# The order of silu, product and weight splits in the expert steps of a decoder kernel

## The chip, the cores and the metric

The kernel runs on one core of a Trainium2 chip. The metric is the device time of one execution in microseconds (us); less is better. Its engines are TensorE (PE, matmul), VectorE (DVE), ScalarE (ACT), GpSimd (POOL) and SyncE (SP), each with a queue of instructions of its own that it works off in order. Semaphores join them.

## The reference

The model is a decoder trunk of two layers for 256 tokens of width 1024, in fp32. Each layer has a mixer, a cross attention and a feed-forward part. The feed-forward part of the second layer is a mixture of 8 experts, of which each token uses two. The change touches only that part:

```python
def swiglu(x, w1, w2):
    gate, up = jnp.split(x @ w1, 2, axis=-1)
    return (jax.nn.silu(gate) * up) @ w2

def moe_ffn(x, router_w, w1, w2):
    ...
    logits = (xt @ router_w).astype(jnp.float32)
    top_logit, top_idx = lax.top_k(logits, TOP_K)
    gates = jax.nn.softmax(top_logit, axis=-1)
    ...
    yb = lax.map(expert_group, (xb, blk_expert)).reshape(cap, d)
    yb = yb * slot_gate[:, None].astype(yb.dtype)
```

An expert's hidden width is 2816, so its weights are 22 chunks of the first product (w1) and 11 of the second (w2), each 128 x 2048 fp32, 1 MB. All 8 experts are 264 chunks.

## The kernel before

**Split weights.** TensorE multiplies fp32 numbers as a sum of products of a high and a low part. ScalarE copies a chunk (`raw`, `kvX`, `arena`) to its high part in one of four homes, three buffers `whi` and one `whi_fourth` (L820, `split_high`). VectorE subtracts this from the chunk and writes the low part over the chunk (L1949, `split_low`). SP's queue loads the chunks into 9 slots. A slot, and a home, come free when TensorE has used the chunk (`w_used`). Some chunks are taken whole, in unsplit fp32 matmuls, and need neither engine.

**Pairs, units and steps.** The experts go in 4 pairs of one full expert (up to 128 tokens, H) and one light expert (up to 64 tokens, L). Each expert is a row of 22 units: units 0 to 10 take two chunks of w1 each and produce gate and up for 256 hidden columns, units 11 to 21 take one chunk of w2. `turns()` gives the steps: in a step comes a unit of the full expert and then the unit of the light expert that stands three behind (LAG), so steps 0 to 2 of a later pair still hold units 19 to 21 of the light expert of the pair before, and the first pair has none there. Chunks are taken whole in the full expert only: the second chunk of units 4, 5, 6, 8 and 9, and the chunks of units 11 to 13. Where this text speaks of step 7, the full expert's unit is 7.

**Splits run four ahead.** The split of a chunk can begin when TensorE is done with the split chunk four places before it in the stream, whose home it takes. `splits_through(n)` issues the splits that follow on the chunks up to n:

```python
while done[0] < NSPLIT and (done[0] < HOMES or SPLIT[done[0] - HOMES] <= n):
    split_high(p, done[0])
    done[0] += 1
```

So in a step ScalarE and VectorE have up to two splits that follow on the full unit's chunks, and up to two that follow on the light unit's.

**What else is in a step.** For the full unit ScalarE makes the silu of the gate half (L1159, `xsilu`), which waits until TensorE has done both chunks of the unit, and VectorE multiplies it by the up half (L2535, `xgated`). TensorE transposes the product behind the next unit (L1762), ScalarE and VectorE copy and split the result (L1131 and L1134, `hidden_hi`; L2505, `hidden_lo`). For the light unit the high and low rows of the 128 come out of the array apart: ScalarE copies the low rows (L1172), VectorE adds them to the high ones (L2552, `lsum`), ScalarE makes the silu of the sum (L1125, `light_silu`) and VectorE the product (L2497, `light_gated`). The two last belong to the step after (`behind`). The transposes of the light product are L1775. At step 1 of the first pair the light expert's tokens are gathered by TensorE (L1619) and copied out (L1100, `first_hi_of("L")`). At steps 5 and 7 of the later pairs TensorE spreads the outputs of the pair before (L1673, L1674) and VectorE adds them to h (L2519). At the end of a light expert ScalarE and VectorE write the high and low part of its output (L1178, L2559).

**TensorE's lines.** The split product of the full expert is L1249 to L1251, 12 matmuls of 512 columns for a chunk of w1; a whole chunk is L1714, 8 matmuls; the light expert's chunk is L1711 and L1712, 8 matmuls, and L1748 and L1749 in its second product. `ready(n)` waits for the low part of a chunk (`lo_ready`).

Of the kernel before, what the change touches and what calls it, by code (L numbers as in the profile page):

```python
# [69 lines left out]
def unit_chunks(u):  # L70
    return (2 * u, 2 * u + 1) if u < NF // 2 else (W1_CHUNKS + u - NF // 2,)
# [87 lines left out]
def build(nc, x, mem, par, con, lvl, lin_w, ffn_w, out):  # L159
# [31 lines left out]
    with ExitStack() as ctx:  # L191
# [546 lines left out]
        def _(act):  # L738
# [340 lines left out]
            def experts(p):  # L1079
# [3 lines left out]
                def splits_through(n):  # L1083
# [4 lines that stand above are left out]
# [57 lines left out]
                    act.wait_ge(routed_ok, 1)  # L1145
                behind = None
                for a, (full, light) in enumerate(turns()):
                    if full:
                        i, u = full
                        splits_through(SIDX["H", i, unit_chunks(u)[-1]])  # L1150
                    if a == 1:
                        first_hi_of("L")
                    if behind:
                        light_silu(*behind)
                        behind = None
                    if full:
                        if u < NF // 2:
                            act.wait_ge(w_used, unit_end(p, "H", i, u))
                            nc.scalar.activation(xsilu[:, u % 2, :], pb[:, u % 2, 0:S], ACT.Silu).then_inc(silu_ready, 1)  # L1159
                        if 1 <= u <= NF // 2:  # L1160
                            hidden_hi(i, u - 1)
                        if u == UNITS - 1:
                            act.wait_ge(selT_ready, nth(p, i))
                            act.wait_ge(w_used, unit_end(p, "H", i, u))
                            nc.scalar.activation(yHh.rearrange("p (a c) -> p a c", a=2), pb[:, 1:3, :], ACT.Copy,
                                                 scale=gs[:, 0:1]).then_inc(yH_hi, 1)
                    if light:
                        i, u = light
                        splits_through(SIDX["L", i, unit_chunks(u)[-1]])
                        if u < NF // 2:  # L1170
                            act.wait_ge(w_used, unit_end(p, "L", i, u))
                            nc.scalar.activation(low_rows[0:LIGHT, :], pb[LIGHT:P, 3 + u % 2, :], ACT.Copy).then_inc(low_ready, 1)  # L1172
                            behind = light
                        if 2 <= u <= NF // 2 + 1:
                            light_hidden_hi(i, u - 2)
                        if u == UNITS - 1 and i < PAIRS_E - 1:
                            act.wait_ge(w_used, unit_end(p, "L", i, u))
                            nc.scalar.activation(yLh.rearrange("p (a c) -> p a c", a=2), pb[:, 4:6, :], ACT.Copy,  # L1178
                                                 scale=gs[:, 1:2]).then_inc(yL_hi, 1)
                    if full:  # L1180
                        i, u = full
                        if u == 9:
                            selections_turned(i)
                        if u in (15, 18) and i < PAIRS_E - 1:
                            gathered_hi(i + 1, (u - 15) // 3)
# [667 lines left out]
        def _(dve):  # L1853
# [616 lines left out]
            def experts(p):  # L2470
# [3 lines left out]
                def splits_through(n):  # L2474

                    while done[0] < NSPLIT and (done[0] < HOMES or SPLIT[done[0] - HOMES] <= n):
                        split_low(p, done[0])
                        done[0] += 1
# [42 lines left out]

                behind = None
                for a, (full, light) in enumerate(turns()):
                    if full:
                        i, u = full
                        splits_through(SIDX["H", i, unit_chunks(u)[-1]])
                    if a == 1:
                        first_lo_of(p, "L")
                    if behind:
                        light_gated(*behind)  # L2530
                        behind = None
                    if full:
                        if u < NF // 2:
                            dve.wait_ge(silu_ready, full_no(p, i, u))
                            V.tensor_tensor(xgated[:, u % 2, :], xsilu[:, u % 2, :], pb[:, u % 2, S:2 * S],  # L2535
                                            ALU.mult).then_inc(g_ready, 1)
                        if 1 <= u <= NF // 2:
                            hidden_lo(i, u - 1)
                        if u == UNITS - 1:
                            dve.wait_ge(yH_hi, nth(p, i))  # L2540
                            V.scalar_tensor_tensor(out=yHl.rearrange("p (a c) -> p a c", a=2), in0=pb[:, 1:3, :],
                                                   scalar=gs[:, 0:1],
                                                   in1=yHh.rearrange("p (a c) -> p a c", a=2).bitcast(F32),
                                                   op0=ALU.mult, op1=ALU.subtract).then_inc(yH_lo, 1)
# [140 lines left out]
```

## Time and profile before

| | |
|---|---|
| time, median of 3 runs | 1419.19 us (1417.68 to 1422.4) |
| the profiled execution | 1417.29 us, span 1415.1 us |
| PE busy | 1384.8 us (98%), 7443 matmuls |
| VectorE busy | 1107.9 us (78%) |
| ScalarE busy | 909.9 us (64%) |
| splits of VectorE in the experts (L1949 wlo<-raw,whi alone) | 73, 2282 ns each |
| loads in the experts | 1024 KB each, 7.5 to 8.0 us from issue to landing |
| granted clock of TensorE over the span | 0.996 |

The span runs from the first to the last instruction; the profiled execution's time is 2.2 us longer. The experts take the second half, from about 709 us to 1407 us. Times of a single instruction are those from its start to its end; instructions of one engine overlap by some 0.1 us, so the distance from one start to the next is shorter than what an instruction takes. A matmul of 512 columns is written as taking 0.39 us and more, while the next starts 0.23 us later.

### The profile page before, as it was taken

To read this page: it belongs to the slowest core of one execution; us is meant where nothing else is said; L and a number is where in the kernel's file an instruction comes from. 1 tells how busy PE (TensorE), PEld (TensorE's weight loads), DVE (VectorE), ACT (ScalarE), POOL (GpSimd) and SP (SyncE) were. 2 spreads that over 40 slices of the span, in tenths; PEclk is the share of its full clock that TensorE was granted. 3 is DMA by queue.
4 is the path that set the end of the run, shared out by engine and by line. 5 is a ranking of instruction groups with operands and counts; after the bars stand their busy time and mean duration, and the time that the engine had idled before them with its cause. 6 is when DMAs were issued, how large, how long until landed. Compare 5 with 4: busy or idle time off the path is not lost.

```text
span 1415.1 us, 18950 instructions
## 1 busy us (share of the span) xinstructions
PE 1384.8 (98%) x7443; PEld 1139.5 (81%) x7443; DVE 1107.9 (78%) x1187; ACT 909.9 (64%) x1008; POOL 52.3 (4%) x58
## 2 busy tenths in 40 slices
PE   7999999999999999999999999999999999999997
PEld 7999898888888998989776768777687767877775
DVE  7868665666645787865588889988899888998897
ACT  6746444555534756344467778877788777877775
POOL 0031000000000022000000000000000000000000
PEclk9999999999999999999999999999999999999998
DMA  8433453455555443353569999999999999999993
GB/s 312 160 127 118 151 177 113 156 179 188 198 181 188 172 146 104 135 178 126 231 240 401 400 400 405 423 402 380 405 404 423 399 376 411 403 423 399 378 414 150
DMA packets 54480, 388.36 MB, mean 274 GB/s; under 512 B 6000, under 2 KB 6256, under 8 KB 8176
## 3 DMA queue, kind: packets, MB, share of 16 engines
q1 hardware_dynamic: 53840, 384.98, 70.3%
q10 hardware_dynamic: 544, 2.10, 0.4%
q8 instruction: 61, 1.00, 0.3%
q14 instruction: 35, 0.29, 0.1%
HBM read 386.00 MB, written 1.05 MB: 274 GB/s over the span
## 4 chain that ended last, share of the span: by engine, by line
issue 51%; PE 47%; DVE 2%; DMA 0%; ACT 0%; POOL 0%; POOLq 0%; DVEq 0%
PE pb L1249 10%; PE pb L1250 10%; PE pb L1251 10%; PE pb L1545 5%; PE pb L1546 3%; PE pb L1397 1%; PE pb L1479 1%; PE pb L1499 1%; PE pb L1230 1%; PE pb L1548 1%; DVE xTb L1919 1%; DMA h<-in_x 0%; PE pb L1489 0%; PE pb L1455 0%; PE pb L1456 0%
## 5 line engine op out<-in xcount | busy, mean ns | idle before, releaser
L1870 DVE TENSOR_TENSOR wlo<-raw,whi 128x2048 fp32r<-128x2048 f32 (+1 forms) x101 | 225.9, 2246 | 107.6 <-ACT whi L750 107.3
L750 ACT ACTIVATE whi<-raw 128x2048 fp32r<-128x2048 f32 (+1 forms) x101 | 189.9, 1882 | 148.9 <-PE pb L1251 116.0
L820 ACT ACTIVATE whi<-raw 128x2048 fp32r<-128x2048 f32 x91 | 172.7, 1913 | 42.3 <-PE pb L1251 29.7
L1949 DVE TENSOR_TENSOR wlo<-raw,whi 128x2048 fp32r<-128x2048 f32 x73 | 165.3, 2282 | 16.8 <-ACT whi L820 16.6
L1249 PE MATMUL pb<-xTb,whi 128*128 128x256 f32 x384 | 110.0, 287 | 1.8 <-DVE xTb L1907 1.2
L1545 PE MATMUL pb<-xTb,whi 128*128 128x512 f32 x308 | 111.0, 399 | 0.2
L1250 PE MATMUL pb<-xTb,whi 128*128 128x256 f32 x384 | 108.6, 283 | 0.0
L1251 PE MATMUL pb<-xTb,wlo 128*128 128x256 f32 x384 | 108.6, 283 | 0.0
L1711 PE MATMUL pb<-whi,xg 128*128 128x512 f32 x264 | 107.1, 406 | 0.0
L1949 DVE TENSOR_TENSOR kvXr<-kvX,whi 128x2048 fp32r<-128x2048 f32 x42 | 95.4, 2282 | 12.1 <-ACT whi L820 12.1
L1546 PE MATMUL pb<-xTb,wlo 128*128 128x256 f32 x352 | 91.6, 281 | 0.0
L820 ACT ACTIVATE whi<-kvX 128x2048 fp32r<-128x2048 f32 x42 | 79.9, 1914 | 16.6 <-PE pb L1251 11.6
L1249 PE MATMUL pb<-whi,xTb 128*128 128x512 f32 (+1 forms) x224 | 86.0, 384 | 0.7 <-DVE xTb L1919 0.6
L820 ACT ACTIVATE whi<-arena 128x2048 fp32r<-128x2048 f32 x41 | 78.0, 1914 | 12.0 <-PE pb L1712 5.3
L1251 PE MATMUL pb<-whi,xTb 128*128 128x512 f32 (+1 forms) x224 | 84.2, 376 | 0.0
L1250 PE MATMUL pb<-wlo,xTb 128*128 128x512 f32 (+1 forms) x224 | 84.1, 376 | 0.0
L1249 PE MATMUL pb<-whi,xg 128*128 128x512 f32 x208 | 82.2, 395 | 0.0
L1251 PE MATMUL pb<-whi,xg 128*128 128x512 f32 x208 | 81.2, 390 | 0.0
L820 ACT ACTIVATE whi_fourth<-raw 128x2048 fp32r<-128x2048 f32 x34 | 65.1, 1914 | 20.2 <-PE pb L1251 10.4
L1249 PEld LDWEIGHTS pb<-xTb,whi 128*128 128x128 f32 x384 | 73.6, 192 | 2.5 <-issue 1.7
L1250 PEld LDWEIGHTS pb<-xTb,whi 128*128 128x128 f32 x384 | 73.6, 192 | 0.1
L1251 PEld LDWEIGHTS pb<-xTb,wlo 128*128 128x128 f32 x384 | 73.6, 192 | 0.0
(459 smaller groups left out, 3488.0 us busy)
## 6 DMA issues: line engine op xcount, KB each, us to landing
raw<-in_ffn_w SPq DMA_DIRECT2D x179, 1024.0 KB, 7.5
raw<-in_lin_w SPq DMA_DIRECT2D x64, 1024.0 KB, 4.9
kvX<-in_ffn_w SPq DMA_DIRECT2D x60, 1024.0 KB, 8.0
arena<-in_ffn_w SPq DMA_DIRECT2D x58, 1024.0 KB, 8.0
raw<-in_lin_w SPq DMA_DIRECT2D x4, 536.0 KB, 5.5
arena<-in_mem ACTq DMA_DIRECT2D x2, 1024.0 KB, 8.1
h<-in_x SPq DMA_DIRECT2D x1, 1024.0 KB, 5.2
out<-xn SPq DMA_DIRECT2D x2, 512.0 KB, 4.0
```

The costliest lines, as they stand in the source:

```text
L750: nc.scalar.activation(whi[:, m % HRING, c], raw[:, m % RING, c], ACT.Copy).then_inc(hi_ready, 1)
L820: nc.scalar.activation(high_home(p, n), xraw_slots[slot], ACT.Copy).then_inc(hi_ready, 1)
L1230: mm = nc.tensor.transpose(pb[:, turn_bank(no, b), i * S + t * P:i * S + (t + 1) * P], xn[:, t, k * P:(k + 1) * P], ident)
L1249: nc.tensor.matmul(o, lh, rh, start=first, stop=False)
L1250: nc.tensor.matmul(o, lh, rl, start=False, stop=False)
L1251: return nc.tensor.matmul(o, ll, rh, start=False, stop=last)
L1397: mm = nc.tensor.matmul(pb[:, b + hd % 2, i * P:(i + 1) * P], K[r, o + t * P:o + (t + 1) * P], Q[r, o + t * P:o + (t + 1) * P], start=True ...
L1545: nc.tensor.matmul(o, high, xTb[:, :, k, :], start=(k == 0), stop=False)
L1546: mm = nc.tensor.matmul(o[:, 0:S], low, xTh[:, k, :], start=False, stop=False)
L1711: nc.tensor.matmul(o, both, w[0][:, kk, :], start=first, stop=False)
L1870: V.tensor_tensor(wlo[:, m % RING, c], raw[:, m % RING, c], whi[:, m % HRING, c].bitcast(F32), ALU.subtract).then_inc(lo_ready, 1)
L1949: V.tensor_tensor(xlo_slots[slot], xraw_slots[slot], high_home(p, n).bitcast(F32), ALU.subtract).then_inc(lo_ready, 1)
```

## The change

In the loop over the steps, on ScalarE and on VectorE, the splits that follow on the full unit's chunks stood first. They now stand behind the full unit's silu (on VectorE: its product). Whatever stood between comes ahead of them too: at step 1 the first gather's parts for the light expert, and in all steps with something `behind`, the light silu and the light product. The splits that follow on the light unit's chunks stay where they were. TensorE, SP and POOL have the same instructions in the same order.

```diff
@@ ScalarE @@
                 for a, (full, light) in enumerate(turns()):
-                    if full:
-                        i, u = full
-                        splits_through(SIDX["H", i, unit_chunks(u)[-1]])
                     if a == 1:
                         first_hi_of("L")
                     if behind:
                         light_silu(*behind)
                         behind = None
                     if full:
+                        i, u = full
                         if u < NF // 2:
                             act.wait_ge(w_used, unit_end(p, "H", i, u))
                             nc.scalar.activation(xsilu[:, u % 2, :], pb[:, u % 2, 0:S], ACT.Silu).then_inc(silu_ready, 1)
+                        splits_through(SIDX["H", i, unit_chunks(u)[-1]])
                         if 1 <= u <= NF // 2:
                             hidden_hi(i, u - 1)
@@ VectorE @@
                 for a, (full, light) in enumerate(turns()):
-                    if full:
-                        i, u = full
-                        splits_through(SIDX["H", i, unit_chunks(u)[-1]])
                     if a == 1:
                         first_lo_of(p, "L")
                     if behind:
                         light_gated(*behind)
                         behind = None
                     if full:
+                        i, u = full
                         if u < NF // 2:
                             dve.wait_ge(silu_ready, full_no(p, i, u))
                             V.tensor_tensor(xgated[:, u % 2, :], xsilu[:, u % 2, :], pb[:, u % 2, S:2 * S],
                                             ALU.mult).then_inc(g_ready, 1)
+                        splits_through(SIDX["H", i, unit_chunks(u)[-1]])
                         if 1 <= u <= NF // 2:
                             hidden_lo(i, u - 1)
```

ScalarE at the start of the experts, steps 0 and 1 of the first pair, before. L820 is a split, L1159 the full unit's silu, L1100 the parts of the light expert's gather, L1131 the copy of the transposed product.

```order
L820 ACTIVATE whi_fourth<-raw 128x2048
L820 ACTIVATE whi<-raw 128x2048 x2
L1159 ACT_TABLE_LOAD
L1159 ACTIVATE xsilu<-pb 128x256
L820 ACTIVATE whi<-arena 128x2048
L820 ACTIVATE whi_fourth<-arena 128x2048
L1100 ACTIVATE xg<-pb,params 128x64 x8
L1159 ACTIVATE xsilu<-pb 128x256
L1131 ACTIVATE arena<-pb 128x256
```

The same place of ScalarE after the change; the silu is now L1157, and its number in the file alone has changed.

```order
L1157 ACT_TABLE_LOAD
L1157 ACTIVATE xsilu<-pb 128x256
L820 ACTIVATE whi_fourth<-raw 128x2048
L820 ACTIVATE whi<-raw 128x2048 x2
L1100 ACTIVATE xg<-pb,params 128x64 x8
L1157 ACTIVATE xsilu<-pb 128x256
L820 ACTIVATE whi<-arena 128x2048
L820 ACTIVATE whi_fourth<-arena 128x2048
L1131 ACTIVATE arena<-pb 128x256
```

The first silu, with the table load ahead of it, has moved up past the three splits of step 0. The two splits of step 1 (`whi<-arena`, `whi_fourth<-arena`) have moved down past the gather's parts and the silu.

ScalarE at step 7 of the first pair, before. L1172 and L1140 end the step before it, L820 with `raw_77` and `kvX` are the two splits that follow on the full unit's chunks, L1125 is the light silu.

```order
L1172 ACTIVATE arena<-pb 64x512
L1140 ACTIVATE xhL<-pb 128x2x64
L820 ACTIVATE whi_fourth<-raw_77 128x2048
L820 ACTIVATE whi<-kvX 128x2048
L1125 ACTIVATE arena<-arena 64x256
L1159 ACTIVATE xsilu<-pb 128x256
L1134 ACTIVATE xhTh<-pb 128x256
L820 ACTIVATE whi<-raw 128x2048 x2
L1172 ACTIVATE arena<-pb 64x512
L1140 ACTIVATE xhL<-pb 128x2x64
```

The same place after the change, where the copy of the low rows is L1171.

```order
L1171 ACTIVATE arena<-pb 64x512
L1140 ACTIVATE xhL<-pb 128x2x64
L1125 ACTIVATE arena<-arena 64x256
L1157 ACTIVATE xsilu<-pb 128x256
L820 ACTIVATE whi_fourth<-raw_77 128x2048
L820 ACTIVATE whi<-kvX 128x2048
L1134 ACTIVATE xhTh<-pb 128x256
L820 ACTIVATE whi<-raw 128x2048 x2
L1171 ACTIVATE arena<-pb 64x512
L1140 ACTIVATE xhL<-pb 128x2x64
```

Both silus now stand ahead of the two splits, and the splits of the light unit (`raw`, x2) stand where they stood.

VectorE at step 7 of the first pair, before. L2552 is the light sum of the step before, L1949 a split, L2497 the light product, L2535 the full unit's product, L2505 the low part of the transposed product.

```order
L2552 TENSOR_TENSOR arena<-arena,pb 64x512
L2511 TENSOR_TENSOR xhL<-pb,xhL 128x2x64
L1949 TENSOR_TENSOR raw8r<-raw_77,whi_fourth 128x2048
L1949 TENSOR_TENSOR kvXr<-kvX,whi 128x2048
L2497 TENSOR_TENSOR arena<-arena 64x256
L2535 TENSOR_TENSOR xgated<-xsilu,pb 128x256
L2505 TENSOR_TENSOR xhTl<-pb,xhTh 128x256
L1949 TENSOR_TENSOR wlo<-raw,whi 128x2048 x2
L2552 TENSOR_TENSOR arena<-arena,pb 64x512
```

The same place after the change; these lines are now L2550, L1948, L2496, L2532 and L2504.

```order
L2550 TENSOR_TENSOR arena<-arena,pb 64x512
L2510 TENSOR_TENSOR xhL<-pb,xhL 128x2x64
L2496 TENSOR_TENSOR arena<-arena 64x256
L2532 TENSOR_TENSOR xgated<-xsilu,pb 128x256
L1948 TENSOR_TENSOR raw8r<-raw_77,whi_fourth 128x2048
L1948 TENSOR_TENSOR kvXr<-kvX,whi 128x2048
L2504 TENSOR_TENSOR xhTl<-pb,xhTh 128x256
L1948 TENSOR_TENSOR wlo<-raw,whi 128x2048 x2
L2550 TENSOR_TENSOR arena<-arena,pb 64x512
```

The two products have come ahead of the two splits.

## Rows read from the trace of the kernel before

In the timelines a row gives start and duration in us, and in brackets how long the engine had been idle and what ended that.

**Rows 1.** Busy time by window; then PEclk, DMA share, GB/s

```profile
721.20:724.40 3.20, 3.17 (x8) 2.50 (x9) 3.20 (x2) 3.17 (x3) 0.00 (x0) 0.50 1.02 430
726.00:1407.00 681.00, 678.51 (x2880) 507.29 (x2880) 613.35 (x528) 523.64 (x513) 0.26 (x1) 1.00 0.97 390
```

**Rows 2.** Waits, 726 to 1407 us. Who waited for whom: us, times, longest

```profile
PE pb L1762 <- DVE xgated L2535: 0.2, 1, 0.2
```

**Rows 3.** Timeline, first steps: start, us, engine, line, [idle <-releaser]

```profile
715.37 1.92 ACT L820 ACTIVATE whi_fourth<-raw 128x2048 fp32r<-128x2048 f32 x1 [4.20 <-DVE small L2440]
...
720.90 1.28 ACT L1159 ACT_TABLE_LOAD   x1
...
718.89 2.28 DVE L1949 TENSOR_TENSOR wlo<-raw,whi_fourth 128x2048 fp32r<-128x2048 f32 x1
...
715.20 0.39 PE L1249 MATMUL pb<-whi,xg 128*128 128x512 f32 x1
...
721.23 0.79 PE L1249 MATMUL pb<-whi_fourth,xg 128*128 128x512 f32 x1 [3.14 <-DVE wlo L1949]
```

**Rows 4.** Timeline, steps 1 to 4 of the first pair

```profile
729.93 1.75 ACT L1100 ACTIVATE xg<-pb,params 128x64 fp32r<-128x64 f32 x8 [2.18 <-PE pb L1619]
...
735.44 0.48 PE L1249 MATMUL pb<-whi,xg 128*128 128x512 f32 x1
...
741.07 0.38 PE L1762 MATMUL pb<-consts,xgated 128*128 128x128 f32 x2
...
744.94 0.39 PE L1249 MATMUL pb<-whi,xg 128*128 128x512 f32 x1
```

**Rows 5.** Timeline, the end of step 7 of the first pair, and step 8

```profile
781.82 1.92 ACT L820 ACTIVATE whi<-kvX 128x2048 fp32r<-128x2048 f32 x1 [0.81 <-PE pb L1251]
783.64 0.40 ACT L1125 ACTIVATE arena<-arena 64x256 f32<-64x256 f32 x1
...
784.47 3.71 ACT L820 ACTIVATE whi<-raw 128x2048 fp32r<-128x2048 f32 x2
...
792.09 0.42 ACT L1125 ACTIVATE arena<-arena 64x256 f32<-64x256 f32 x1 [1.18 <-DVE arena L2552]
...
783.77 2.29 DVE L1949 TENSOR_TENSOR kvXr<-kvX,whi 128x2048 fp32r<-128x2048 f32 x1 [0.29 <-ACT whi L820]
...
786.98 4.48 DVE L1949 TENSOR_TENSOR wlo<-raw,whi 128x2048 fp32r<-128x2048 f32 x2
791.38 0.67 DVE L2552 TENSOR_TENSOR arena<-arena,pb 64x512 f32<-64x512 f32 x1
...
781.55 0.39 PE L1762 MATMUL pb<-consts,xgated 128*128 128x128 f32 x2
...
785.84 0.50 PE L1249 MATMUL pb<-whi_fourth,xg 128*128 128x512 f32 x1
```

**Rows 6.** Timeline, steps 0 to 4 of the second pair

```profile
887.63 1.92 ACT L820 ACTIVATE whi<-raw 128x2048 fp32r<-128x2048 f32 x1 [0.72 <-PE pb L1251]
...
889.18 0.39 PE L1249 MATMUL pb<-whi,xg 128*128 128x512 f32 x1
...
902.24 0.38 PE L1762 MATMUL pb<-consts,xgated 128*128 128x128 f32 x2
...
904.30 0.39 PE L1249 MATMUL pb<-whi,xg 128*128 128x512 f32 x1
...
909.75 0.38 PE L1762 MATMUL pb<-consts,xgated 128*128 128x128 f32 x2
...
913.65 0.39 PE L1249 MATMUL pb<-whi,xg 128*128 128x512 f32 x1
...
909.19 1.28 DVE L2559 SCALAR_TENSOR_TENSOR yLl<-pb,route,yLh 128x1024 fp32r<-128x1024 f32 x1
```

**Rows 7.** Timeline, another gap of TensorE

```profile
105.81 1.17 PE L1397 MATMUL pb<-arena 64*128 64x128 f32 x17
108.10 1.16 PE L1397 MATMUL pb<-arena 64*128 64x128 f32 x15 [1.13 <-DVE arena L2143]
```

## The prediction

> **What bounds the kernel now.** I read the busy time by window first. Over 681 us of the experts, TensorE is busy for 678.5 us at the full clock, while VectorE has work for 613 us of it and ScalarE for 524 us [rows 1]. A busy share is not yet a bound, so the waits came next: from 726 us to the end of the experts TensorE waits once for another engine, 0.2 us, and that is the product that the change brings forward [rows 2]. Last came the timeline. Ahead of this stretch is the one real wait of TensorE, 3.1 us before 721.23, for the low part of a weight chunk [rows 3]. ScalarE, VectorE and the loads feed TensorE just in time, and nobody sees them. So in the experts a change can take away at most these waits, and whatever makes TensorE wait anew is paid in full.
>
> **What the change moves.** No instruction is added or removed. Three things come ahead of the splits of the full expert's chunks: the light expert's silu and product left from the step before, the full expert's own silu and product, and at step 1 the parts of the light expert's first gather. The silu waits for the last matmul of the full expert's unit. The first split of the step waited only for the unit's first chunk, one chunk (2.7 to 3.4 us) earlier. Now ScalarE holds it behind the silu. No DMA stands in the moved code: SP's queue waits for TensorE alone, and POOL has nothing here.
>
> **What the silu itself brings.** The product is wanted by the transposes that follow the next unit of the full expert, almost a step later. The bound on the gain is the 0.2 us that TensorE waits for it once [rows 2]. I take 0.2 us, and it is in the first term below.
>
> **What the late splits cost.** First the durations. A release by TensorE is seen by ScalarE 0.27 us after the next matmul's start (781.55 to 781.82). A split is handed to VectorE after 1.92 + 0.03 us (781.82 to 783.77). Small operations of ScalarE follow each other 0.28 us apart (three of them from 783.64 to 784.47). VectorE's splits follow each other 2.20 us apart (two from 786.98 to 791.38) and one lasts 2.29 us; between 783.77 and 786.98 stand one split and three small operations, so these take 0.34 us each. VectorE's sum for the light expert lasts 0.67 us, and ScalarE sees it 0.04 us later (791.38 to 792.09) [rows 5]. TensorE starts 0.06 us after VectorE's split ends (718.89 + 2.28 = 721.17 to 721.23) [rows 3].
>
> So the first split of a step is ready, at the earliest, 0.27 + 0.28 + 1.92 + 0.03 + 2.29 + 0.06 = 4.85 us after the end of the full unit. The splits run four split chunks ahead, since there are four homes for high parts. Where no chunk between is taken whole, the fourth one on comes up soon. I went through the steps and asked when each is wanted; U is the end of the full unit, and the lag is what TensorE has lost so far.
>
> First pair, steps 0 and 1. ScalarE comes at 715.37 and sees the end of unit 0 (715.20) at 715.47. Table load (1.28), silu (0.28) and the split (1.92) end at 718.95, and VectorE is busy with the routing until 718.89. Its product of 0.34 us now stands ahead of the split that TensorE waits for: some 0.3 us more at 721.23 [rows 3]. The 0.2 us wait for the product behind unit 1 goes away. Lag 0.1 us.
> First pair, step 1. The two splits now stand behind the parts of the gather, which wait for TensorE until 729.93. Eight parts (1.6 us), lag, silu (0.27) lead to 731.9; the first split is ready 1.92 + 0.04 + 2.28 + 0.06 us later, at 736.2. Unit 3 wants it at 735.44 + 0.1 [rows 4]. Stall 0.65 us, lag 0.75.
> First pair, step 3. Ready at U + 4.85, wanted by unit 4 at U + 3.87 (741.07 to 744.94) [rows 4]. Stall 1.0 us, lag 1.7.
> First pair, step 7. Here it is no longer U that decides. ScalarE's light silu waits for VectorE's sum, and that is the end of VectorE's work for the step before; the next splits stand behind it. Both engines so work in series: 0.04 + 0.28 + 0.28 + 1.92 + 0.03 = 2.55 us from the sum's end to VectorE's first split, then 3 splits (6.6), one small operation (0.34) and the sum (0.67): 10.2 us a step with three splits. In step 3 VectorE's first split starts at 741.07 + 0.75 + 2.50 = 744.3 and four splits and the sum lead to 753.8. Steps 4, 5 and 6 end with the sum at 784.3. The first split of step 7 is ready at 784.3 + 2.55 + 2.29 + 0.06 = 789.2; unit 8 wants it at 785.84 + 1.7 = 787.55 [rows 5]. Stall 1.65 us. Step 10 also has four splits, but three whole chunks follow and its first split is wanted a step later: no stall.
> First pair: 0.1 + 0.65 + 1.0 + 1.65 = 3.4 us.
>
> Each later pair, step 0. U is 887.63 - 0.27 = 887.36. The second chunk of unit 1 is wanted half a unit (5.45 / 2, 904.30 to 909.75) after 889.18, at U + 4.55; ready at U + 4.85. Stall 0.3 us.
> Each later pair, steps 2 and 3. Step 2 has three splits and the low part of the previous light expert's output. With U = 902.24 + 0.3, VectorE's first split starts at 905.04, three splits end at 911.64, the low part (1.28 - 0.08) at 912.84, the product of step 3 (0.34) at 913.18, the split at 915.46: ready 915.5. Unit 4 wants it at 913.65 + 0.3 [rows 6]. Stall 1.55 us. In steps 5 and 7 TensorE also spreads outputs, 8 matmuls ahead of the next unit, and that covers step 7's split.
> Each later pair 1.85 us, three of them: 5.5 us.
>
> Sum: 3.4 + 5.5 = 8.9 us. The profiled execution took 1417.3 us, so it would take 1426.2; the median of the three runs is 1.9 us above it, so the forecast is 1419.2 + 8.9 = **1428.1 us**. The runs shown spread over 4.7 us, and about 0.3% (4.3 us) is what a measurement can tell from no change.
>
> The bounds: if every chain is 0.3 us shorter than I think, the nine stalls (3 in the first pair, 2 in each other) lose 2.7 us: 1425.4. If each is 0.3 us longer, and step 2's first split in the later pairs stalls as well (U + 4.85 again, 907.4, and its need half a unit after 904.30 + 0.3, 907.3), it is 1432.
>
> **The rivals.**
> Series pace (15%). The chain of step 7 holds in the later pairs too, and step 10's reaches TensorE. For it speaks that VectorE has 90% of work already, so idle time is hard to make up [rows 1]; against it the 1.9 us of cover that spreading gives. Another 1.65 us at step 7 of three pairs and up to 1 us at step 10 of four: +9, 1437.
> The clock (8%). After the 3.1 us wait the granted clock was 0.50 for 3.2 us: 8 matmuls filled it, 0.40 us each, where 24 take 5.45 us (904.30 to 909.75), 0.23 each: 1.4 us lost [rows 1, 3, 6]. If the five stalls of 1 us and more cost this too, it is 5 x 1.4 = 7 more, 1435. Against it: after a gap of 1.13 us, 15 matmuls took 1.16 us, the pace of the 17 before it, 1.17 us [rows 7]. My stalls lie nearer to the 1.13 than to the 3.1. The Trainium skill (TensorE: Matmul & The Clock Gate, Part 1) has it that the clock is full or half according to how busy TensorE has just been; the trace agrees with both levels, 1.00 (2.4 GHz) and 0.50 (1.2 GHz), and that rule speaks against any change that opens gaps in a full queue.
> Absorbed, not slower (14%). The weight stream may be what really sets the pace: the loads fill 0.97 of the DMA time at 390 GB/s. Then late matmuls only use up time that loads would have cost, and it stays at 1419. It decides if the stream can go no faster; against it, TensorE waits for no load, and for 3.2 us the stream did 430 GB/s, 10% more [rows 1, 2]. Slack of 0.3 us at each hand-over and 1.7 at step 7 would do it as well.
> Faster (4%). The silu brings back more than the late splits cost. There is 0.2 us of wait to take away in the experts, and the 3.1 us wait ends with VectorE's routing; 1415 would need matmuls that run closer together.
>
> **How the numbers follow.** Forecast 59%: 1424 to 1432. Series 15%, clock 8%, absorbed 14%, faster 4%. The range goes from the top of the absorbed case up to the costly ones: 1422 to 1436. It leaves out most of "absorbed", "faster", and the upper half of "series", some 2 in 10. Slower by over 0.3% (above 1423.5): forecast, series, clock and a little less, 0.81. Within: 0.15. Faster: 0.04.
>
> **What would show it.** In the trace after, TensorE should show new waits for VectorE's low parts, behind units 2, 3 and 7 of the first pair and behind units 0 and 3 of the other three, 9 us in all, against 3.3 us now with the one at 721 us still there. ScalarE should wait longest for the unit's end ahead of the silu and for VectorE's sum ahead of the light silu, no longer ahead of the splits. The clock should stay at 1.00. I am wrong if the waits are there and the time is not, if they stand at other steps, or if they are of another size.

## The result

The changed kernel takes 1438.8 us (median of 4 runs, 1438.4 to 1442.7) against 1419.3 us before; the ratio is 1.0144, with a 95% interval of 1.0122 to 1.0165. It is slower by 19.5 us. The forecast was slower by 8.9, with a range that ended at 1436.

The page of the profile after, its span, its busy times and the group that has changed most:

```profile
span 1437.0 us, 18951 instructions
...
PE 1392.0 (97%) x7443; PEld 1140.1 (79%) x7443; DVE 1109.9 (77%) x1187; ACT 902.6 (63%) x1008; POOL 52.3 (4%) x58
...
L1125 ACT ACTIVATE arena<-arena 64x256 f32<-64x256 f32 x44 | 18.4, 417 | 126.6 <-DVE arena L2550 126.6
```

The span is 21.9 us longer (1437.0 against 1415.1), while VectorE and ScalarE do the same work. What ScalarE's light silu (L1125) waits for VectorE has become the longest wait of that engine in the experts. From 726 us to their end, before and after (engine, line, waited for: us, times, longest):

```profile
ACT arena L1125 <- DVE arena L2552: 35.9, 19, 3.0
...
ACT arena L1125 <- DVE arena L2550: 126.6, 44, 3.8
```

The splits stand behind this silu in ScalarE's queue now and are held with it. Their own waits for TensorE have fallen from 84.6 to 16.5 us. VectorE and TensorE over the stretch of [rows 1] (columns as there):

```profile
726.00:1407.00 681.00, 666.78 (x2798) 492.82 (x2797) 596.37 (x514) 504.93 (x499) 0.00 (x0) 0.99 0.98 388
```

TensorE is busy for 666.8 us of the 681 where it was for 678.5. Its waits up to 1429 us, where there was one of 0.2 us [rows 2]:

```profile
PE pb L1248 <- DVE kvXr L1948: 3.3, 3, 1.3
PE pb L1774 <- DVE xhL L2510: 3.0, 4, 0.8
PE pb L1248 <- DVE wlo L1948: 2.4, 2, 1.3
PE pb L1248 <- DVE raw7r L1948: 2.4, 2, 1.3
PE pb L1248 <- DVE raw8r L1948: 1.8, 1, 1.8
PE pb L1248 <- DVE raw6r L1948: 1.2, 1, 1.2
```

These are 13 waits, 14.1 us. L1248 is the full expert's matmul; L1774 are the light expert's transposes. Where they stand is read in the timeline, of which these are the waits of the first pair and one of the second, behind the one that was there before (start, us, engine, line, idle before and what ended it):

```profile
721.83 0.50 PE L1248 MATMUL pb<-whi_fourth,xg 128*128 128x512 f32 x1 [3.45 <-DVE wlo L1948]
...
747.79 0.47 PE L1248 MATMUL pb<-whi,xg 128*128 128x512 f32 x1 [0.82 <-DVE kvXr L1948]
...
790.63 0.47 PE L1248 MATMUL pb<-whi_fourth,xg 128*128 128x512 f32 x1 [1.77 <-DVE raw8r L1948]
...
832.72 0.30 PE L1774 MATMUL pb<-consts,arena 64*128 64x64 f32 x2 [0.76 <-DVE xhL L2510]
...
870.48 0.47 PE L1248 MATMUL pb<-whi_fourth,xhTh 128*128 128x512 f32 x1 [1.11 <-DVE kvXr L1948]
...
924.23 0.47 PE L1248 MATMUL pb<-whi,xg 128*128 128x512 f32 x1 [1.26 <-DVE wlo L1948]
```

747.79 is the start of unit 4, which began at 744.94 before [rows 4], 790.63 that of unit 8, before 785.84 [rows 5], and 924.23 that of unit 4 in the second pair, before 913.65 [rows 6]. So TensorE is 2.85, 4.8 and 10.6 us late at these three places. The starts at 832.72 (the light transposes of step 11) and 870.48 (unit 18) are waits that the prediction does not have.

I set the same matmuls of both traces side by side to see how the 21.9 us come about. Unit 4 loses 1.0 us in the first pair and 1.45 in each other, 5.4; unit 8 of the first pair 1.7; the transposes of step 11 lose 0.8 in each pair, 3.2; unit 18 loses 1.2 to 1.4 in each, 5.1; units 0 to 3 of the later pairs lose 0.6 each, 1.8; the start 0.3. Two stretches at the half clock cost 3.0 (below). That is 20.5 us; the rest is spread in small pieces, 0.3 us of it ahead of the experts. All this holds for the two profiled executions; one of the two stretches does not come in each execution (last section).

### The profile page after: what moved, and what is told of

Same layout as the page of the kernel before. It is cut to its first block, busy times and chain, and to the rows that moved or that the text cites. A ratio compares the mean times of both kernels' runs of the same rounds, so it can differ in the third digit from the quotient of the medians.

```text
span 1437.0 us, 18951 instructions
## 1 busy us (share of the span) xinstructions
PE 1392.0 (97%) x7443; PEld 1140.1 (79%) x7443; DVE 1109.9 (77%) x1187; ACT 902.6 (63%) x1008; POOL 52.3 (4%) x58
## 4 chain that ended last, share of the span: by engine, by line
issue 51%; PE 44%; DVE 2%; DMA 1%; ACT 0%; POOL 0%; POOLq 0%; DVEq 0%; ACTq 0%
PE pb L1248 10%; PE pb L1250 9%; PE pb L1249 9%; PE pb L1544 5%; PE pb L1545 3%; PE pb L1396 1%; PE pb L1478 1%; PE pb L1498 1%; PE pb L1547 1%; DMA arena<-in_mem 1%; PE pb L1229 1%; DVE xTb L1918 1%; DVE wlo L1869 0%; DMA h<-in_x 0%; PE pb L1488 0%
## 5 line engine op out<-in xcount | busy, mean ns | idle before, releaser
L1948 DVE TENSOR_TENSOR wlo<-raw,whi 128x2048 fp32r<-128x2048 f32 x73 | 164.9, 2284 | 17.1 <-ACT whi L820 17.1
L820 ACT ACTIVATE whi<-raw 128x2048 fp32r<-128x2048 f32 x91 | 171.9, 1908 | 5.9 <-PE pb L1250 5.8
L1248 PE MATMUL pb<-xTb,whi 128*128 128x256 f32 x384 | 110.2, 287 | 2.4 <-DVE xTb L1906 1.2
L1948 DVE TENSOR_TENSOR kvXr<-kvX,whi 128x2048 fp32r<-128x2048 f32 x42 | 95.4, 2285 | 11.6 <-ACT whi L820 11.6
L1125 ACT ACTIVATE arena<-arena 64x256 f32<-64x256 f32 x44 | 18.4, 417 | 126.6 <-DVE arena L2550 126.6
L1248 PE MATMUL pb<-whi,xg 128*128 128x512 f32 x208 | 83.9, 403 | 4.7 <-DVE kvXr L1948 2.1
L1248 PE MATMUL pb<-whi,xTb 128*128 128x512 f32 (+1 forms) x224 | 85.8, 383 | 0.7 <-DVE xTb L1918 0.6
L820 ACT ACTIVATE whi<-kvX 128x2048 fp32r<-128x2048 f32 x42 | 79.5, 1908 | 4.0 <-PE pb L1250 3.9
L820 ACT ACTIVATE whi<-arena 128x2048 fp32r<-128x2048 f32 x41 | 77.7, 1910 | 0.3 <-PE pb L1250 0.3
L1248 PEld LDWEIGHTS pb<-xTb,whi 128*128 128x128 f32 x384 | 73.6, 192 | 3.3 <-issue 2.5
L1948 DVE TENSOR_TENSOR wlo<-raw,whi_fourth 128x2048 fp32r<-128x2048 f32 x28 | 64.0, 2286 | 13.3 <-ACT whi_fourth L820 13.3
```

What stands on the lines that cost most here:

```text
L820: nc.scalar.activation(high_home(p, n), xraw_slots[slot], ACT.Copy).then_inc(hi_ready, 1)
L1125: nc.scalar.activation(lsilu[0:LIGHT, :], lsum[0:LIGHT, 0:S], ACT.Silu).then_inc(lsilu_ready, 1)
L1248: nc.tensor.matmul(o, lh, rh, start=first, stop=False)
L1948: V.tensor_tensor(xlo_slots[slot], xraw_slots[slot], high_home(p, n).bitcast(F32), ALU.subtract).then_inc(lo_ready, 1)
```

## The experiments

Each kernel was timed beside the kernel before on the same chip. In what follows a ratio is to that kernel, with its interval; 0.01 is 14.2 us. The changed kernel itself was not timed again beside them, so "less than the changed kernel" is the difference of two ratios, each known to some 2 to 4 us. Differences of 5 us and less are therefore not sure by the times alone; what the text says of single waits rests on the traces. U is the end of the full unit, as in the prediction.

**1. One engine at a time.** Two kernels: ScalarE has the changed order and VectorE the old one, and the other way round.

```diff
 # ScalarE alone: VectorE's loop keeps
+                    if full:
+                        i, u = full
+                        splits_through(SIDX["H", i, unit_chunks(u)[-1]])
                     if a == 1:
                         first_lo_of(p, "L")
```

> ScalarE has the changed order, VectorE the old one (its splits first, then the products). Theory A (the high parts are late: on ScalarE the first split of a step stands behind the unit's end and behind VectorE's light sum): nearly the whole loss, as the low parts cannot start before the high ones; only the 0.3 to 0.7 us of the two products ahead of VectorE's splits are saved at each stall, so 12 to 19 us over before. Theory B (VectorE, the fuller engine, stands idle for its products ahead of its splits): at most 5 us over before.

Measured: 1465.2 us, ratio 1.0324 (1.0291 to 1.0357), 46 us more than before. Neither theory had that. TensorE's waits from 709 us on, its largest:

```profile
PE pb L1761 <- DVE xhTl L2504: 6.5, 4, 2.1
PE pb L1774 <- DVE arena L2496: 6.4, 4, 1.7
...
PE pb L1761 <- DVE xgated L2534: 5.0, 2, 4.8
...
PE pb L1774 <- DVE xhL L2510: 3.3, 3, 1.1
```

With VectorE's splits in front, its products stand behind splits whose high parts are late, and then TensorE waits for the products themselves (L2496, L2534) and for the low part of the transposed product (L2504). Of the four lines shown, the changed kernel has only the wait for the copy of the light transposes (L2510).

> VectorE has the changed order, ScalarE the old one. Theory A as such, that only late high parts matter: at most 5 us over before. Theory B: most of the loss or more, since VectorE's splits now stand behind a product whose silu follows on both high splits of the step: first low part ready at U + 5.7 us instead of U + 4.85 (U is the full unit's end), 15 to 30 us over before.

Measured: 1444.0 us, ratio 1.0165 (1.0135 to 1.0196), 26 us by the medians. That is the range of theory B, and theory A's bound of 5 us falls. But B falls by the first run. ScalarE's order alone costs more than twice what the two together do; VectorE's alone costs about the same as both (its interval, 1.0135 to 1.0196, overlaps 1.0122 to 1.0165). The reading is that the products and the splits should stand in the same order on both engines, because each hands work to the other in that order; the first run shows it for the old order on VectorE alone. The loss cannot be put down to one engine.

**2. One half of the change at a time.** The full expert's silu and product ahead of the splits, everything else behind them; and the reverse.

```diff
 # the full expert's alone, ScalarE (VectorE likewise)
                     if full:
                         i, u = full
+                        if u < NF // 2:
+                            act.wait_ge(w_used, unit_end(p, "H", i, u))
+                            nc.scalar.activation(xsilu[:, u % 2, :], ...
                         splits_through(SIDX["H", i, unit_chunks(u)[-1]])
                     if a == 1:
                         first_hi_of("L")
                     if behind:
                         light_silu(*behind)
```

> Only the full expert's silu and product stand ahead of the splits, the light ones and the first gather's parts stay behind them, on both engines. If the two mechanisms are apart (the wait for the unit's end delays the first split of a step; the light silu's wait for VectorE's sum puts both engines in series): new waits of TensorE ahead of unit 4 in all pairs (1.0 to 1.5 us), unit 8 of the first pair (0.6) and in unit 1 of the later pairs (0.3), none ahead of the light expert's transposes of step 11 and none ahead of unit 18; 6 to 9 us over before. If one backlog makes all stalls, they stay where they are in the changed kernel and the loss is over 14 us.

Measured: 1430.6 us, ratio 1.0080 (1.0055 to 1.0104), 11 to 13 us more than before. TensorE's waits:

```profile
PE pb L1777 <- DVE xhL L2513: 4.3, 4, 1.1
PE pb L1251 <- DVE kvXr L1951: 2.1, 2, 1.3
PE pb L1251 <- DVE raw7r L1951: 1.3, 1, 1.3
```

The waits ahead of unit 4 are there (0.81 us in the first pair, 1.30 in the second) and ahead of unit 8 (0.51), and none ahead of unit 18. But the transposes of step 11 wait too, 1.1 us each, where the expectation had none, and the loss is above its 6 to 9 us. So the full expert's silu alone is enough for this wait.

> Only the light silu and product, and the first gather's parts at step 1, stand ahead of the splits; the full expert's silu and product stay behind. If the series of the two engines is a mechanism of its own: waits of TensorE ahead of the transposes of step 11 and ahead of unit 18 in every pair, none ahead of unit 4, and 5 to 10 us over before. If the light silu does harm only together with the full one: under 3 us.

Measured: 1428.6 us, ratio 1.0069 (1.0042 to 1.0095). TensorE's waits:

```profile
PE pb L1764 <- DVE xgated L2537: 3.0, 1, 3.0
PE pb L1777 <- DVE xhL L2513: 1.1, 1, 1.1
PE pb L1251 <- DVE kvXr L1951: 1.1, 1, 1.1
```

The waits ahead of unit 18 are there (1.10 us in the first pair, 0.58 to 0.72 in the others) and none ahead of unit 4, as expected. Unit 8 of the first pair waits 0.39. Ahead of the transposes of step 11 there is one only, in the first pair. A new one of 3.0 us stands at step 1: the gather's parts are ahead of the splits, and the product of unit 1 is behind them. The two halves are mechanisms of their own in units 4 and 18. The sum 0.0080 + 0.0069 = 0.0149 is near the 0.0144 of the whole, but not because the places add up: the wait of 3.0 us is in the light half alone, step 11 waits in both, and unit 8 waits 0.51 and 0.39 apart and 1.8 together.

**3. The places, one by one.** These kernels are the changed one with the old order put back at some steps, on both engines. The condition differs: step 14; step 10; step 2; steps 0 (of the later pairs), 3 (of all) and 7 (of the first); those with 14 and the copy of step 11 first as well; and steps 0, 2, 3, 7, 10 and 14.

```diff
                 for a, (full, light) in enumerate(turns()):
+                    if full and full[1] == 14:    # or other steps
+                        splits_through(SIDX["H", full[0], unit_chunks(full[1])[-1]])
                     if a == 1:
```

> The changed kernel, but at step 14 alone the full unit's split stands ahead of the light silu and product, as before the change. If the light silu at step 14 starts the lateness that reaches unit 18: the four waits of 1.2 to 1.4 us ahead of unit 18 go, 5 us less than the changed kernel (1.1% over before in place of 1.4%). If they come from the backlog of steps 10 to 13, they stay and so does the time.

Measured: ratio 1.0109 (1.0081 to 1.0138), 5.0 us less than the changed kernel's 1.0144. The waits ahead of unit 18 are gone in all four pairs, those of unit 4, unit 8 and step 11 stand as they were. In the changed kernel step 14 looks like this in the first pair, ScalarE first and then VectorE:

```profile
854.78 0.42 ACT L1125 ACTIVATE arena<-arena 64x256 f32<-64x256 f32 x1 [2.42 <-DVE arena L2550]
855.11 1.90 ACT L820 ACTIVATE whi_fourth<-arena 128x2048 fp32r<-128x2048 f32 x1
...
857.04 2.29 DVE L1948 TENSOR_TENSOR raw6r<-arena,whi_fourth 128x2048 fp32r<-128x2048 f32 x1 [1.32 <-ACT whi_fourth L820]
...
866.26 1.88 DVE L2486 SCALAR_TENSOR_TENSOR xg<-pb,params,xg 128x128 fp32r<-128x128 f32 x8
868.06 2.28 DVE L1948 TENSOR_TENSOR kvXr<-kvX,whi_fourth 128x2048 fp32r<-128x2048 f32 x1
```

L1125 at 854.78 is the light silu, which had waited 2.4 us for the sum, and the split of step 14 follows at 855.11. VectorE has it at 857.04, and from there on its splits and the gather's low parts (L2486) follow each other without a gap up to the split at 868.06. Its end at 870.34 is what unit 18 waits for. Four steps lie between the cause and the wait.

> The changed kernel, but with the old order at step 10 alone, the step with four splits ahead of the waits of step 11. If VectorE's backlog that shows at steps 11, 12 and at unit 18 begins here: the waits of step 11 go and the ones ahead of unit 18 shrink too, 4 to 7 us less than the changed kernel. If it has built up over steps 4 to 9: the waits stay, time within 1 us of the changed kernel.

Measured: ratio 1.0113 (1.0098 to 1.0129), 4.4 us less. The waits of step 11 are gone, and the ones ahead of unit 18 are down from 1.1 or 1.2 us to between 0.2 and 0.4. The backlog begins at step 10. It and step 14 both have to be in the new order for unit 18 to lose its full 1.3 us: step 10 put back takes away 0.8 to 0.9 of it, step 14 put back all. This is step 10 of the first pair in the changed kernel:

```profile
820.34 0.38 ACT L1157 ACTIVATE xsilu<-pb 128x256 f32<-128x256 f32 x1 [0.83 <-PE pb L1250]
...
832.41 0.42 ACT L1125 ACTIVATE arena<-arena 64x256 f32<-64x256 f32 x1 [3.30 <-DVE arena L2550]
...
822.56 4.49 DVE L1948 TENSOR_TENSOR wlo<-raw,whi 128x2048 fp32r<-128x2048 f32 x2 [1.38 <-ACT whi L820]
826.97 0.42 DVE L2504 TENSOR_TENSOR xhTl<-pb,xhTh 128x256 fp32r<-128x256 f32 x1
827.30 2.28 DVE L1948 TENSOR_TENSOR raw6r<-arena,whi_fourth 128x2048 fp32r<-128x2048 f32 x1
...
831.71 0.67 DVE L2550 TENSOR_TENSOR arena<-arena,pb 64x512 f32<-64x512 f32 x1
832.30 0.27 DVE L2510 TENSOR_TENSOR xhL<-pb,xhL 128x128 fp32r<-128x128 f32 x1
```

Unit 10's silu starts at 820.34, the first of four splits reaches VectorE at 822.56, the sum follows at 831.71 and the copy of the light transposes (L2510) ends at 832.57. TensorE's next transposes want that copy, and start at 832.72.

> The changed kernel, but at step 10 the copy of the light expert's transposes (ScalarE's high part, VectorE's low part) stands ahead of the light unit's splits and not behind them and the light sum. It takes away what TensorE waits for ahead of the light transposes of step 11. If each stall is a deadline of its own: the four waits of 0.8 us go, 3 us less than the changed kernel. If VectorE carries one backlog from step 10 to unit 18: the waits of step 11 go and those ahead of unit 18 grow by as much, no change in time against the changed kernel (within 1 us).

Measured: ratio 1.0145 (1.0125 to 1.0166), no gain. The edit makes the copy that step 11 waits for ahead of the splits of the light unit 7 (shown on ScalarE, VectorE likewise):

```diff
+                        if u == 7:    # u is the light unit
+                            light_hidden_hi(i, u - 2)
...
-                        if 2 <= u <= NF // 2 + 1:
+                        if u != 7 and 2 <= u <= NF // 2 + 1:
```

The four waits of step 11 went, but they did not show up ahead of unit 18 either. They came one step later, at the transposes of step 12, and are longer:

```profile
PE pb L1776 <- DVE xhL L2512: 4.6, 4, 1.2
```

The waits ahead of unit 18 stayed at 1.1 to 1.2 us. So neither reading came true as it stands. The deadline is no single one: VectorE is late as a whole, and here what was brought forward in its queue put off the copy of the next step.

> The changed kernel, but with the old order (the splits first) at step 3 of all pairs, step 7 of the first and step 0 of the others, the places where the prediction had its stalls. If they are what was forecast there: the waits ahead of unit 4, of unit 8 in the first pair and in unit 1 go, with the slow clock behind unit 8's: 1.0 + 1.7 + 1.5 + 3 x 1.8 = 9.6 us less than the changed kernel. The waits of step 11 and unit 18 stay.

Measured: ratio 1.0090 (1.0070 to 1.0111), 7.7 us less, where 9.6 were expected. In the first pair unit 4 and unit 8 no longer wait. In the later pairs unit 4 still waited 0.94 to 0.99 us of its 1.3 (the 1.1 in the next expectation is too high), although step 3 had the old order.

> The changed kernel, but with the old order at step 2 of the later pairs alone. The earlier run with the old order at step 3 still had TensorE wait 1.1 us ahead of unit 4 in the later pairs. If that wait is made in step 2 (VectorE starts its three splits and the low part of the light output late and hands the lateness on): the three waits ahead of unit 4 in the later pairs shrink from 1.25 us to under 0.5, 3 to 4 us less than the changed kernel. If both steps make it alone (either is enough): they stay above 1 us and the time falls by less than 1 us.

Measured: ratio 1.0138 (1.0122 to 1.0153), 0.9 us less. The waits ahead of unit 4 in the later pairs shrank to about 0.8 us. Either of steps 2 and 3 makes most of the wait alone, so the second reading is the nearer one.

> The three edits (copy first at step 10, old order at step 14, old order at steps 0, 3 and 7) together. If the places named are all: 17 to 18 us less than the changed kernel, 2 us over before, of which 1.5 are the clock at 730 us. If stalls taken away only come back at other steps, it stays at 5 us or more over before, with new waits.

Measured: ratio 1.0073 (1.0050 to 1.0096), 10 us less, not 17. The transposes of step 12 wait 1.2 us in each pair, and unit 4 in the later pairs 1.0. That is the second reading: what the copy's new place took away at step 11 came back at step 12.

> The changed kernel, but with the old order at steps 2, 3, 10 and 14 of every pair, step 7 of the first and step 0 of the others, so at every step where a wait was traced to. If these steps are the whole cause: 0 to 2 us over before, of it up to 1.5 us the half clock near 730 us, and no wait of 1 us behind step 3. If each reordered step leaves some lateness that VectorE hands on: 4 us or more over before, with waits at steps that had none.

Measured: ratio 1.0021 (1.0003 to 1.0040), 3 us over before. The shortest runs, 1421.5 against 1417.5 us, are 4.0 apart, and the profiled executions 4.4 (spans of 1419.5 and 1415.1 us). TensorE's waits, of which the first holds the one of 3.1 us that was there before (now 3.5):

```profile
PE pb L1250 <- DVE wlo L1950: 3.9, 2, 3.5
...
PE pb L1763 <- DVE xgated L2536: 0.3, 1, 0.3
```

No wait of 1 us is left behind step 3. Of the 4.4 us about 1.5 are the half clock near 730 us, 0.5 the wait for the product of step 2 at 743.29 us, and 2.0 unit 4 of the later pairs, which loses almost 0.7 in each (it waits 0.4). The result lies between the two readings: the steps named are the cause of the loss apart from some 2.5 us, and that is what the other reordered steps leave.

**4. The other direction.** In the trace before, TensorE has one real wait in the experts, for a low part behind the routing's arithmetic [rows 3]. The next kernel is the one before without it.

```diff
                 first_hi_of("H")
-                if p == 0:
-                    act.wait_ge(routed_ok, 1)
...
             first_lo_of(0, "H")
             split_low(0, 2)
+            split_low(0, 3)
...                      # VectorE's experts()
-                done = [HRING if p == 0 else HOMES]
+                done = [HOMES]
```

> Not the change but the kernel before with its one real wait in the experts taken away: ScalarE no longer waits for the routing's flag ahead of the fourth split but only ahead of reading it at the end, and VectorE makes the fourth low part ahead of the routing's arithmetic and not behind it. If the 3.1 us wait and the half clock behind it (1.4 us) are lost time of their own: 4.5 us less than before, 1415, about 0.3%. If the routing, 2.2 us later, then makes someone else wait (the expert numbers for SP's queue, the light selection for TensorE), or the weight stream sets the pace: no gain, 1418 to 1420.

Measured: 1423.7 us, ratio 1.0042 (1.0028 to 1.0056), slower by 6 us, which neither reading had. The wait for weights is gone, and a longer one is there for the product of unit 0. TensorE, then VectorE:

```profile
726.08 0.69 PE L1761 MATMUL pb<-consts,xgated 128*128 128x128 f32 x2 [5.16 <-DVE xgated L2535]
...
721.21 4.48 DVE L1948 TENSOR_TENSOR wlo<-raw,whi 128x2048 fp32r<-128x2048 f32 x2
725.61 0.41 DVE L2535 TENSOR_TENSOR xgated<-xsilu,pb 128x256 f32<-128x256 f32 x1
```

VectorE makes two splits from 721.21 on and the product only at 725.61. The window behind it shows the half clock for 12 us (start:end us, length, busy of PE, PEld, DVE, ACT, POOL, PEclk, DMA, GB/s):

```profile
726.00:738.00 12.00, 11.92 (x45) 10.95 (x46) 6.38 (x12) 2.29 (x10) 0.00 (x0) 0.50 0.51 217
```

So here is a place where TensorE does wait for the product, and there the change was tried alone, on top of the last kernel (the difference to it is shown):

```diff
                 first_hi_of("H")
+                if p == 0:
+                    split_high(0, HRING)    # and done = [HOMES] on ScalarE too
...
                     if full:
                         i, u = full
-                        splits_through(SIDX["H", i, unit_chunks(u)[-1]])
+                        if a:
+                            splits_through(SIDX["H", i, unit_chunks(u)[-1]])
...                      # silu, on VectorE the product
+                        if a == 0:
+                            splits_through(SIDX["H", i, unit_chunks(u)[-1]])
```

> The kernel before with its start mended further: the fourth split's high and low part ahead of the routing as in the last run, and now at step 0 of the first pair alone the full silu and product ahead of the other splits, which is the change at the one step where TensorE waits for the product. The last run traded 3.1 us of waiting for 5.2 us at the transposes of unit 0's product. If the product's place was the reason: that wait falls to under 1 us, the clock stays full, and it is 3 to 4 us less than before, 1414 to 1416. If VectorE's routing and splits are simply too much work ahead of unit 2: the wait moves on to unit 2, and the time stays within 0.3% of before.

Measured: 1415.1 us (12 runs, 1414.7 to 1417.6) against 1422.3 (23 runs, 1417.5 to 1425.8), ratio 0.9964 (0.9950 to 0.9979). It beats both kernels, and its span, 1412.8 us, is 8.2 us shorter than that of the last one, whose product stands behind the splits. The product's new place was not tried without the fourth split's. The product comes at 721.66, ahead of the two splits, and TensorE waits 0.7 us:

```profile
722.12 0.44 PE L1766 MATMUL pb<-consts,xgated 128*128 128x128 f32 x2 [0.74 <-DVE xgated L2541]
...
721.66 0.41 DVE L2541 TENSOR_TENSOR xgated<-xsilu,pb 128x256 f32<-128x256 f32 x1
721.98 4.49 DVE L1953 TENSOR_TENSOR wlo<-raw,whi 128x2048 fp32r<-128x2048 f32 x2
```

The clock was to stay full, and did not: it was 0.74 from 726 to 732 us. The wait is 2.4 us shorter than that of [rows 3], and so the span, 1412.8 us against 1415.1, is 2.3 shorter. The rest of the 7 us between the medians is not explained: the kernel before spreads over 8 us in these runs, this one over 3.

## Why the prediction was wrong

**Bound and direction.** Right. From 726 us on TensorE had nothing to win but 0.2 us, and each new wait was paid in full.

**The forecast stalls.** The large terms were well sized. For unit 4 it had 1.0 us in the first pair and 1.55 in the others; measured 1.0 and 1.45. For unit 8 it had 1.65; measured 1.7. At unit 1 to 3 of the later pairs it had 0.3; measured 0.6. With 0.3 at the start, where it had 0.1, this is 9.2 us together where the forecast had 8.9. That the sums come so near is partly luck: the 0.65 us of unit 3 are missing in it, and the later pairs lost 0.9 more than forecast in their first units. Step 7 of the later pairs was covered, as forecast: no unit 8 waits there. This is step 7 in the changed kernel, where ScalarE and VectorE were to work in series:

```profile
785.67 0.42 ACT L1125 ACTIVATE arena<-arena 64x256 f32<-64x256 f32 x1 [2.88 <-DVE arena L2550]
785.99 0.36 ACT L1157 ACTIVATE xsilu<-pb 128x256 f32<-128x256 f32 x1
786.26 1.90 ACT L820 ACTIVATE whi_fourth<-raw 128x2048 fp32r<-128x2048 f32 x1
...
784.96 0.67 DVE L2550 TENSOR_TENSOR arena<-arena,pb 64x512 f32<-64x512 f32 x1
...
788.19 2.29 DVE L1948 TENSOR_TENSOR raw8r<-raw,whi_fourth 128x2048 fp32r<-128x2048 f32 x1 [1.26 <-ACT whi_fourth L820]
```

The sum starts at 784.96, the light silu at 785.67, the silu at 785.99, the split at 786.26, and VectorE's split at 788.19: 3.2 us from the sum's start, 2.55 from its end (784.96 + 0.67), the same as forecast. The stall of 0.65 us at unit 3 cannot be seen in this trace: TensorE was late there already by the half clock. It is seen in three of the experiments, whose order at the start is the changed one and which were at full clock there (steps 14 and 2 old, copy first). TensorE loses 0.6 us, the size forecast, but not for the split: the transposes ahead of unit 3 wait for ScalarE's copy (L1131), which stands behind both splits. With step 2 old:

```profile
736.12 0.41 PE L1763 MATMUL pb<-consts,xgated 128*128 128x128 f32 x2 [0.53 <-ACT arena L1131]
```

**The step that failed** is this one: "Step 10 also has four splits, but three whole chunks follow and its first split is wanted a step later: no stall." It asked only when the splits' own results are wanted. Behind step 10's four splits VectorE also has the sum and the copy of the light transposes, and the transposes of step 11 wait for that copy: 0.8 us in each pair, 3.2 together. The run with step 10 put back showed it.

**A term that was left out** is step 14, the last with a light silu ahead of a split. Its split starts behind VectorE's sum, and VectorE has no gap until unit 18, where the lateness comes out: 1.2 to 1.4 us in each pair, 5.1 together. The run with step 14 put back took away just these. They need step 10 too: with it put back, two thirds of them went. The prediction went through no step behind 10. The rival of the series pace, at 15%, was the nearest: the same mechanism, with 1437 as its time. Its "up to 1 us at step 10 of four" came, as 0.8; its 1.65 us at step 7 of three pairs did not; and it has no step 14 either, so its time fits by luck.

**The clock** was given 8% as a rival of its own and held in small part. Of the eight waits of 1 us and more one alone, that of 1.8 us, had the half clock behind it, 1.5 us. Another 1.5 us came near 730 us with no new wait ahead of it. So in the profiled execution 3.2 + 5.1 + 3.0 = 11.3 us were missing from the sum.

**The range** was too narrow at the top for a mechanism that made TensorE wait at two more places in each pair than I had found. The rivals "absorbed" and "faster" had nothing in them. The stream is no limit: it moved 388 GB/s over the experts after against 390 before [rows 1], and 421 in a window of 3.5 us (the last section).

What is still open: why unit 4 of the later pairs keeps most of its wait when step 2 or step 3 alone is put back was not taken apart further. When both are (and step 0 with them), 0.4 us stay.

## What to carry to other kernels

Where an engine is never waited for, an instruction of its queue that is brought forward can win nothing, and everything that it passes may lose. When two engines hand work to each other in a fixed order, follow a late instruction through the whole queue of the second one, up to its next gap, and hold every result behind it against its own deadline, the small ones too. A reordering that is bad in a steady loop can be right at the one step where the trace shows a wait for its result (shown here with the fourth split brought forward too). And if both engines' orders are to change, change them together: here the new order on ScalarE alone cost more than twice as much as on both.

## What the runs showed of the hardware

TensorE's half clock did not only follow the long waits. These are windows of the changed kernel:

```profile
729.80:733.20 3.40, 3.40 (x12) 2.72 (x12) 1.18 (x7) 2.96 (x10) 0.00 (x0) 0.53 0.22 89
...
791.50:795.00 3.50, 3.50 (x10) 2.75 (x9) 3.50 (x3) 3.20 (x4) 0.00 (x0) 0.52 1.00 421
924.00:928.00 4.00, 3.77 (x15) 2.84 (x16) 4.00 (x3) 3.57 (x3) 0.00 (x0) 1.00 1.01 422
```

And this is the first of them in the kernel with step 14 old, whose order is the same up to there:

```profile
729.80:733.20 3.40, 3.40 (x19) 2.90 (x19) 0.85 (x5) 2.63 (x10) 0.00 (x0) 1.00 0.36 152
```

The clock was about half from 729.8 to 733.2, although TensorE had been busy there since 721.8, with small matmuls of 64 columns (the gather) from 726 on. But with the same instructions it was full there with step 14 old, and also with step 2 old and with the copy first; so this stretch comes in some executions and not in others, and no run here shows what makes it come, or that it is a cost of the change. It was half again behind the wait of 1.8 us that ended at 790.63, from 791.5 to 795, but full behind the wait of 1.3 us that ended at 924.23, as behind the other waits of 1.3 us and less. The Trainium skill (TensorE: Matmul & The Clock Gate, Part 1) has the clock follow how busy TensorE has just been; the two levels agree with it (0.53 and 0.52 are windows nearly all at 1.2 GHz, 1.00 is 2.4 GHz). Each of the two stretches at half clock cost about 1.5 us.
